# Hybrid HGRN2 and pooling block: the w_out combinations move to GpSimd's DMA queue, the staged rows load in two groups, the last two output pairs run their products in order 1 to 7

## The reference, cut to what matters

```
h = rms_norm(z)
q, fz, iv, g_hg, u, g_pool, m_hg, m_pool = split(h @ w_in + b_in)      # eight 1024-wide parts
o = hgrn2_chunkwise(q, k, iv, log_f)                                   # gated linear recurrence
y_hg   = (rms_norm(o) * silu(g_hg)) @ w_down_hg
y_pool = (pool_mix(u) * pool_scale * silu(g_pool)) @ w_down_pool
merged = sigmoid(m_hg) * y_hg + sigmoid(m_pool) * y_pool
out    = rms_norm(z + merged @ w_out)[16:]
```

## Time and profile before

| | before |
|---|---|
| median of 3 runs | 1046.86 us (1046.70, 1046.86, 1048.11) |
| time of the profiled execution | 1046.04 us |
| its span, first to last instruction | 1044.3 us |
| TensorE, matmul | 1016.9 us busy, 97% of the span |
| VectorE | 812.2 us, 78% |
| ScalarE | 510.8 us, 49% |
| GpSimd | 100.3 us, 10% |
| mean granted clock of TensorE | 0.998 |

### The profile page before, as it was taken

One profiled execution on the slowest core, in us unless ns is written; L12 is line 12 of the kernel. 1 busy time (PEld: TensorE's weight loads), 2 busy tenths in 40 slices (PEclk: granted clock), 3 DMA queues, 4 the chain that ended last, 5 costly groups with the idle time before them and its releaser, 6 DMA issues.

```text
span 1044.3 us, 18526 instructions
## 1 busy us (share of the span) xinstructions
PE 1016.9 (97%) x7204; PEld 829.0 (79%) x7204; DVE 812.2 (78%) x1319; ACT 510.8 (49%) x860; POOL 100.3 (10%) x162
## 2 busy tenths in 40 slices
PE   7999999999999999999999999999998999999996
PEld 7767888888888888878888887788776888788875
DVE  7989787868696968787666877875659879988975
ACT  7764636363636353544353433444337436435664
POOL 6200000001010101010101010011101010000130
PEclk9999999999999999999999999999999999999999
DMA  7221111111020202121312222229662384658373
GB/s 276 51 81 63 42 62 42 62 35 68 24 81 21 82 21 83 41 82 52 101 41 91 61 91 81 71 83 341 241 229 100 119 339 145 217 183 333 70 176 106
DMA packets 42630, 117.17 MB, mean 112 GB/s; under 512 B 4752, under 2 KB 4752, under 8 KB 42544
## 3 DMA queue, kind: packets, MB, share of 16 engines
q1 hardware_dynamic: 27904, 78.72, 22.8%
q0 software_dynamic: 8976, 26.26, 7.9%
q10 hardware_dynamic: 5664, 11.02, 3.0%
HBM read 86.62 MB, written 29.36 MB: 111 GB/s over the span
## 4 chain that ended last, share of the span: by engine, by line
PE 77%; DVE 14%; issue 4%; DMA 2%; ACT 2%; POOL 0%; SPq 0%; DVEq 0%; ACTq 0%
PE acc L1596 63%; PE levels L1649 2%; DVE w_lo L1872 2%; PE miscs L1671 1%; PE miscs L1683 1%; PE miscs L1682 1%; DVE r_lo L2428 1%; PE acc L1538 1%; PE levels L1596 1%; PE miscs L1478 1%; PE levels L1478 1%; DVE att L2029 1%; DMA comb_spill<-comb 1%; DVE qx L2048 1%; PE miscs L1689 1%
## 5 line engine op out<-in xcount | busy, mean ns | idle before, releaser
L1596 PE MATMUL acc<-r_hi,w_hi 128*128 128x512 f32 x1200 | 333.1, 400 | 11.8 <-ACT first L1001 4.5
L1596 PE MATMUL acc<-r_lo,w_hi 128*128 128x512 f32 x1200 | 329.5, 394 | 0.5 <-DVE r_lo L2428 0.4
L1596 PE MATMUL acc<-r_hi,w_lo 128*128 128x512 f32 x1200 | 322.2, 390 | 0.5 <-DVE w_lo L1872 0.5
L1596 PEld LDWEIGHTS acc<-r_hi,w_hi 128*128 128x128 f32 x1200 | 218.2, 188 | 61.8 <-ACT first L1001 5.4
L1596 PEld LDWEIGHTS acc<-r_lo,w_hi 128*128 128x128 f32 x1200 | 223.8, 188 | 53.8 <-issue 4.9
L1596 PEld LDWEIGHTS acc<-r_hi,w_lo 128*128 128x128 f32 x1200 | 225.5, 188 | 48.9 <-DVE w_lo L1872 1.0
L911 ACT ACTIVATE w_hi<-sum 128x512 fp32r<-128x512 f32 x164 | 102.9, 628 | 170.6 <-DVE sum L1905 91.5
L1872 DVE TENSOR_TENSOR w_lo<-sum,w_hi 128x512 fp32r<-128x512 f32 x164 | 111.9, 687 | 51.9 <-ACT w_hi L911 51.5
L1872 DVE TENSOR_TENSOR w_lo<-raws,w_hi 128x512 fp32r<-128x512 f32 x120 | 82.0, 686 | 50.0 <-ACT w_hi L911 49.9
L911 ACT ACTIVATE w_hi<-raws 128x512 fp32r<-128x512 f32 x120 | 74.6, 624 | 26.0 <-PE acc L1596 23.2
L1001 ACT ACTIVATE second<-acc,bias 128x512 f32<-128x512 f32 x31 | 21.2, 683 | 57.6 <-PE acc L1596 57.6
(11 more groups left out here) (312 smaller groups left out, 1305.2 us busy)
## 6 DMA issues: line engine op xcount, KB each, us to landing
raws<-in_wstream SPq DMA_DIRECT2D x80, 512.0 KB, 3.6
xin<-in_x SPq DMA_DIRECT2D x8, 512.0 KB, 6.3
a_spill<-gt POOLq DMA_DIRECT2D x16, 256.0 KB, 3.5
c_spill<-pg POOLq DMA_DIRECT2D x16, 256.0 KB, 2.7
stage<-a_spill ACTq DMA_DIRECT2D x4, 1024.0 KB, 15.4
comb<-in_wstream SPq DMA_DIRECT2D x4, 1024.0 KB, 5.6
smh_spill<-zq POOLq DMA_DIRECT2D x16, 256.0 KB, 3.2
comb_spill<-comb SPq DMA_DIRECT2D x4, 1024.0 KB, 4.0
```

The source lines that it names most:

```text
L1596: ins = pe.matmul(bank[:, :], weights, moving, start=n == 0 and i in (0, 1, y_first), stop=n == 3 * KH - 1, skip_group_check=True)
```

## The change

Five edits. (1) `load_comb` and `store_comb` move, unchanged but for the engine, from SyncE's queue to GpSimd's, between the gate stores of pairs 26 to 29, and the sums of the pieces move to pairs 27 to 30. (2) `load_stage(0, ...)` goes out in two groups of two, after product 3 of pairs 28 and 29, instead of four after product 3 of pair 27. (3) V5's sum moves one or two products forward (pair 30: after product 3 instead of 5; pair 34: after product 3 instead of 4). (4) In `change`, `add_22(p)` stands ahead of `operand_low(R_B21)`. (5) Pairs `OUT+2` and `FINAL` run in order 0 to 6, with the orders of the copies, additions, sums and squares on the engines to match.

```
-OUT_SUMS += [(p, s) for p in (OUT + 2, FINAL) for s in (S1, S2, S4, S3)]
+OUT_SUMS += [(p, s) for p in (OUT + 2, FINAL) for s in (S1, S2, S3, S4)]
-ORDER += [(p, i) for p in (OUT + 2, FINAL) for i in OUT_ORDER]
+ORDER += [(p, i) for p in (OUT + 2, FINAL) for i in range(PRODUCTS)]
-ADD_ORDER += [(p, c) for p in (OUT + 2, FINAL) for c in (11, 12, 22)]
+ADD_ORDER += [(p, c) for p in (OUT + 2, FINAL) for c in (11, 22, 12)]
-COPY_ORDER += [(p, c) for p in (OUT + 2, FINAL) for c in (1, 5, 2)]
+COPY_ORDER += [(p, c) for p in (OUT + 2, FINAL) for c in (1, 2, 5)]
-SQUARES += [(p, n, t) for p in (OUT + 2, FINAL) for n, t in ((0, 0), (0, 1), (1, 1), (1, 0))]
+SQUARES += [(p, n, t) for p in (OUT + 2, FINAL) for n, t in QUARTERS]
...
-COMB_AT = {(P_MH, 1): (0, 0), (P_MH, 2): (0, 1), (P_MH + 1, 0): (1, 0), (P_MH + 1, 1): (1, 1),
-           (P_MH + 1, 4): (2, 0), (P_MH + 1, 5): (2, 1), (P_MH + 2, 2): (3, 0), (P_MH + 2, 3): (3, 1)}
+COMB_AT = {(P_MM + 1, 3): (0, 0), (P_MM + 1, 4): (0, 1), (P_MH, 1): (1, 0), (P_MH, 2): (1, 1),
+           (P_MH + 1, 0): (2, 0), (P_MH + 1, 1): (2, 1), (P_MH + 1, 6): (3, 0), (P_MH + 2, 0): (3, 1)}
+COMB_DMA = {(P_MM, 3): -1, (P_MM + 1, 0): 0, (P_MH, 0): 1, (P_MH, 3): 2, (P_MH + 1, 3): 3}

 SyncE
-                if (p, n) == (P_MH, 0):
-                    load_comb(0)
-                elif (p, n) in ((P_MH, 1), (P_MH + 1, 0), (P_MH + 1, 1)):
-                    k = 2 * (p - P_MH) + n - 1
-                    store_comb(k)
-                    load_comb(k + 1)
-                elif (p, n) == (P_MH + 2, 0):
-                    store_comb(3)
 GpSimd
             for p in range(P_MM, P_DH):
                 for x in range(4):
                     store_spill(p, x)
+                    if (p, x) in COMB_DMA:
+                        k = COMB_DMA[p, x]
+                        if k >= 0:
+                            store_comb(k)
+                        if k < 3:
+                            load_comb(k + 1)
...
-            residual(OUT + 2, 0, 1)
             residual(OUT + 2, 1, 1)
+            residual(OUT + 2, 0, 1)
 ScalarE
-                    elif i == 3 and p == P_MM + 1:
-                        side_area_free(act)
-                        for x in range(4):
-                            act.wait_ge(spill_stored[x], 16 * STORES_OF[P_MM, x])
-                        for n in range(4):
-                            load_stage(0, n)
...
             for p in range(P_MH, LAST):
                 for i in range(PRODUCTS):
                     during(p, i)
+                    if p in (P_MH, P_MH + 1) and i == 3:
+                        if p == P_MH:
+                            side_area_free(act)
+                            for x in range(4):
+                                act.wait_ge(spill_stored[x], 16 * STORES_OF[P_MM, x])
+                        load_stage(0, 2 * (p - P_MH))
+                        load_stage(0, 2 * (p - P_MH) + 1)
...
             copy_first(FINAL)
+            high(POS[FINAL, 4])
+            square_z(p, 1, 1)
+            square_z(p, 0, 1)
             high(POS[FINAL, 5])
             square_z(p, 1, 0)
+            copy_second(FINAL)
+            high(POS[FINAL, 6])
+            row_left(4)
+            square_z(FINAL, 0, 0)
             copy_fifth(FINAL)
             row_left(5)
+            square_z(FINAL, 1, 1)
             square_z(FINAL, 0, 1)
             root_z(6)
             row_left(6)
 VectorE
                 use(p, 0)
+                add_22(p)
                 operand_low(f, R_B21)
                 ahead(p, 4)
-                add_22(p)
                 ahead(p, 5)
...
-                    if p == P_DH - 2 and i in (5, 6):
-                        stage_sum(0, R_V5 if i == 5 else R_V7)
+                    if p == P_DH - 2 and i in (3, 6):
+                        stage_sum(0, R_V5 if i == 3 else R_V7)
...
             low(POS[FINAL, 0])
+            add_22(OUT + 2)
+            low(POS[FINAL, 1])
             add_12(OUT + 2)
...
             write_right(5)
+            add_22(FINAL)
+            add_residual(1, 1)
+            weigh_left(7)
             add_12(FINAL)
             add_residual(0, 1)
             scale_from_root(6)
-            add_22(FINAL)
             write_right(6)
-            add_residual(1, 1)
-            weigh_left(7)
             final_quarter()
```

More of the change, by code:

```diff
@@ L842, in _, with load_comb, store_comb @@
                                    pg[:, k // 2, (k % 2) * HALF:(k % 2 + 1) * HALF]).then_inc(c_stored[k], 16)
+            out_blocks = wstream[2 * N_PAIRS:2 * N_PAIRS + 8].rearrange("(b s) p c -> s p b c", s=2)
+            def load_comb(k):
+                if k == 0:
+                    side_area_free(pool)
+                else:
+                    pool.wait_ge(S["comb_stored"], 16 * k)
+                pool.dma_start(comb[:, :, :], out_blocks[k // 2][:, :, k % 2 * HALF:(k % 2 + 1) * HALF]) \
+                    .then_inc(S["comb_loaded"], 16)
+            def store_comb(k):
+                pool.wait_ge(S["comb_made"], k + 1)
+                pool.dma_start(comb_dram[:, k // 2].rearrange("b p c -> p b c")[:, :, k % 2 * HALF:(k % 2 + 1) * HALF],
+                             comb[:, :, :]).then_inc(S["comb_stored"], 16)
             for p in range(P_MM, P_DH):
@@ L1466, in _ @@
             row_left(6)
-            square_z(FINAL, 1, 1)
             square_z(FINAL, 1, 0)
@@ L2375, in mixed, with comb_sums @@
                 dve.tensor_tensor(v, mix_banks[k], v, ALU.mult).then_inc(S["c_made"], 1)
+            def comb_sums(k, part):
+                v5_, v4_, v7_, v6_ = (comb[:, n, :] for n in range(4))
+                dve.wait_ge(S["comb_loaded"], 16 * k + 16)
+                if part == 0:
+                    steps.mark(dve.tensor_tensor(v5_, v5_, v7_, ALU.subtract))
+                    steps.mark(dve.tensor_tensor(v7_, v6_, v7_, ALU.subtract))
+                    return
+                steps.settle()
+                steps.mark(dve.scalar_tensor_tensor(v6_, v5_, -1.0, v6_, ALU.mult, ALU.subtract))
+                steps.settle()
+                dve.scalar_tensor_tensor(v4_, v6_, -1.0, v4_, ALU.mult, ALU.subtract).then_inc(S["comb_made"], 1)
             for g in range(5):
@@ L2515, in change @@
                 use(q, 0)
-            def comb_sums(k, part):
-                v5_, v4_, v7_, v6_ = (comb[:, n, :] for n in range(4))
-                dve.wait_ge(S["comb_loaded"], 16 * k + 16)
-                if part == 0:
-                    steps.mark(dve.tensor_tensor(v5_, v5_, v7_, ALU.subtract))
-                    steps.mark(dve.tensor_tensor(v7_, v6_, v7_, ALU.subtract))
-                    return
-                steps.settle()
-                steps.mark(dve.scalar_tensor_tensor(v6_, v5_, -1.0, v6_, ALU.mult, ALU.subtract))
-                steps.settle()
-                dve.scalar_tensor_tensor(v4_, v6_, -1.0, v4_, ALU.mult, ALU.subtract).then_inc(S["comb_made"], 1)
             for p in range(P_MH, P_DH - 1):
@@ L2732, in _ @@
             write_right(3)
+            token_sum(FINAL, S3)
             token_sum(FINAL, S4)
-            token_sum(FINAL, S3)
             low(POS[FINAL, 0])
+            add_22(OUT + 2)
+            low(POS[FINAL, 1])
             add_12(OUT + 2)
-            low(POS[FINAL, 1])
-            add_22(OUT + 2)
             weigh_left(4)
+            low(POS[FINAL, 2])
             low(POS[FINAL, 3])
-            low(POS[FINAL, 2])
-            low(POS[FINAL, 5])
+            low(POS[FINAL, 4])
             add_11(FINAL)
             add_residual(0, 0)
-            low(POS[FINAL, 4])
+            low(POS[FINAL, 5])
             mean_z(4)
```

55 lines of the change are left out of this document (19 added, 36 removed).

## The result

The changed kernel takes **1051.10 us** (median; 1050.07 to 1051.95), the kernel before, in the same comparison, 1046.70: ratio 1.0041 [1.0029, 1.0053]. The prediction was 1039.9, with 1037.4 to 1044.0 as its range: wrong in size and in sign. What came is close to its rival *Slower* (1049 to 1051), which had a chance of 0.07.

A forecast was written before the change was run, and what follows sets the result against it. TensorE computes 1016.9 of 1044.3 us, so only its idle time can be gained. Terms -8.28 + 0.6 + 0.5 + 1.25 + 0.4 - 1.45 = -7.0 gave median 1039.9 us, range 1037.4 to 1044.0.

The forecast's parts named there:

- Slower: Rival: GpSimd transfers over 2 us longer than SyncE's, V5's sum late, gaps in pairs 27, 29, 30; 1049 to 1051, chance 0.07.
- Comb's DMAs leave SyncE's queue: Pairs 28 to 31: raw block lands some 10 us ahead of need, TensorE's gaps go; up to -8.28 us.
- The price on GpSimd's queue: Each 512-row comb transfer takes d longer on GpSimd's queue than SyncE's; d between 0.2 and 1.8, taken as 0.8 us.
- The chain of pieces: Pairs 27 to 30: eight comb transfers in series, last store lands at 770.0, V5's sum 0.3 late; +0.5 us.
- the split `load_stage` costs nothing: Staged loads in two groups cost nothing: V5 needs the first half 35 us after its issue; four loads took 15.4.
- The gate stores at no cost: Pairs 27 to 29: gate stores wait up to 8 us behind comb DMAs, but are needed one pair (19 us) later.
- The first piece: Pair 27: load lands at 712.0, `add_22(27)` ends at 715.95, product 6 wants it at 715.44; +0.6 us.
- The operand changes: First change bound by VectorE's low parts, +1.25 us; second, VectorE idles with `add_22` first, +0.4 us.
- The end: Last two pairs in order 0 to 6 hide `add_22`; `final_quarter` starts at 1036.25, not 1037.70: -1.45 us.
- V5's sum after 771 behind comb_spill: Sign in the later profile that the forecast is wrong: V5's sum (L2437) comes after 771, waiting behind comb_spill.
- issues of comb of over 2 us: Sign in the later profile that the forecast is wrong: comb issues on GpSimd's queue take over 2 us.
- Later pieces: Rival: transfers 1.2 us or more longer on GpSimd, or staged loads hold them; TensorE stopped; 1041.8 to 1046, chance 0.18.

The follow-up runs named there:

- queue_only: Kernel before with only the comb DMAs moved to GpSimd's queue, sums and staged loads where they were: 1050.15 us, ratio 1.0041.
- three_buffers: Changed kernel with three comb buffers instead of one, the second group of staged loads waiting for stores 1 and 2: 1039.43 us, ratio 0.9931.
- after_on_sync: Changed kernel with the eight comb DMAs back on SyncE's queue at the times GpSimd issues them, still one buffer: 1060.88 us, ratio 1.0143.
- spills_first: Changed kernel with each next piece's load behind the pair's four gate stores instead of ahead of three of them: 1054.32 us, ratio 1.0075.
- stage_together: Changed kernel with all four staged loads back after product 3 of pair 27: 1049.00 us, ratio 1.0025.
- three_later_stage_later: Changed kernel with three comb buffers, first piece's sums two products later, second group of staged loads after product 6 of pair 29: 1038.17 us, ratio 0.9919.
- stage_later: Changed kernel with the two groups of staged loads later, after product 3 of pair 29 and product 0 of pair 30: 1052.53 us, ratio 1.0059.

## Why the prediction was wrong, by its steps

**Comb's DMAs leave SyncE's queue (-8.28): right as a mechanism.** The wait ahead of pair 31's weights is gone in the changed kernel and in queue_only. But taking the comb DMAs off the queue gained nothing by itself, since VectorE's waits for comb took its place; the gain came with the second buffer, and then on either queue. With three buffers pair 32 starts at 795.43, and the prediction's -8.28 + 0.6 + 0.5 on 802.61 gives 795.43 too. That agreement is partly luck: the 0.5 for V5 isn't lost there, and the timeline of three_buffers is 0.26 us late at 705 already.

**The price on GpSimd's queue (d = 0.8): too high.** It is 0.2 to 0.4; the row of 128-row issues times four was no guide, an issue of 512 rows takes 0.76 us. The Trainium skill (DMA: Bandwidth & Descriptors, Latency and other measured facts) would have given 0.4, and the traces agree with it (4.4 and 4.5 against 4.0 and 4.3 us). d wasn't the cause: without it, in after_on_sync, the eight transfers took 62.2 us.

**The chain of pieces (+0.5): this step failed.** It said that eight transfers take 38.4 us, the staged loads add about 6, d adds 6.4: 50.8. They took 61.0. With d at 0.4 this is 22.6 - 8 x 0.4 = 19.4 us more than the medians, where 6 was allowed. The last store landed at 781.8 instead of 770.0.

The neighbours of each transfer say roughly where the 19.4 went (an estimate, against 6.0 us for a load and 4.4 for a store). Store 1, store 2 and load 3 ran beside the staged loads and took 12.4, 7.0 and 8.7: 13.3 us of it. This is the term that was mis-sized, and the sentence that the split `load_stage` costs nothing looked only at V5's need of it. The other 6.1 us had no term at all. 3.9 of it is load 1, with three gate stores right behind it and a raw block just ahead (720.03). queue_only shows this part without any staged load: seven transfers 9.7 us longer than in the kernel before, of which seven times 0.4 is d.

The mistake was to take the medians of the earlier trace rows as the price of a transfer. The trace of the kernel before has another price, in its one comb load that ran beside staged loads; the view of that line shows it, and the median hides it:

```profile
L655 SPq DMA_DIRECT2D comb<-in_wstream x4: 368/373/568, 710.5 to 762.9; - x4
...
DMA to landing us min/median/max: 5.1/5.6/15.0
```

Load 0, issued at 710.5 right behind the four staged loads of 708 to 710, took 15.0 us; the other three, from 733 on, took 5.1 to 5.7. In the kernel before nobody was stopped by load 0 but VectorE for 2.5 us (its sums come at 725.5). The change puts the staged loads beside the middle of the chain, and VectorE behind each link of it. The loss then didn't fall on V5 alone (1.63 us at 785.33), where the prediction looked for it, but on every pair with a comb sum: VectorE waited 28.0 us in four places, TensorE 1.04, 1.71, 2.78, 1.70 and 1.63, and part of pair 29 ran at the lower clock.

What stays open is how a transfer's time follows from its neighbours: the runs show that it does, and no run takes the gate stores or the raw blocks away alone.

**The gate stores at no cost: held for whoever needs them, not for the chain.** From 700 to 800 us of the changed kernel no instruction waits for a gate store. But by spills_first the burst behind a load costs that load about 1 us.

**The first piece (+0.6): 1.04 in the changed kernel**, 0.55 to 1.44 in the versions with its place and with the staged loads behind it. In stage_together, where they are back in pair 27, the gaps there are 2.50 and 0.15. Load 0 took 6.9 where 6.4 was counted.

**The operand changes (+1.25, +0.4).** From pair 32's first row to the last gap of the second change the changed kernel takes 904.15 - 807.22 = 96.93 us, the kernel before 897.86 - 802.61 = 95.25: 1.7 more, where 1.65 was forecast. The size is partly luck, for the places were others: 0.73 ahead of ScalarE's copy at 813.55, then 0.40 and 0.38 at r_lo. Another 0.9 us came behind it, with a gap of 0.58 at 924.49 that no step had.

**The end (-1.45): right.** The shift against before is 998.10 - 990.89 = 7.21 us at TensorE's row that stands ahead of the last products, and 1043.56 - 1037.70 = 5.86 at `final_quarter`: -1.35. The timeline of VectorE, which answers to the earlier trace rows:

```profile
1042.90 0.75 DVE L2643 SCALAR_TENSOR_TENSOR z<-z,z_rs,fnw 128x512 f32<-128x512 f32 x1
1043.56 0.68 DVE L2659 SCALAR_TENSOR_TENSOR z<-acc,xr 128x512 f32<-128x512 f32 x1
```

**The rivals.** *Slower* had nearly the right place (the last store at 782 against its 785, losses in pairs 27, 29 and 30, besides one in 28) and the wrong reason: it decided "from d = 2", and got its small chance by d. Of the signs that the prediction named for being wrong, V5's sum after 771 behind comb_spill (781.78) and the gaps in pairs 29 and 30 came; issues of comb of over 2 us did not (0.76). The sum of *Slower* doesn't reach its place either: at d = 2 it gives 705.6 + 58.05 + 16 = 779.7, and 785 needs d = 2.7. The total of the chain decided, and d was only one of three things in it. *Later pieces* had named the other one, staged loads that hold the transfers longer, but priced it by d as well.

## What to carry to other kernels

A chain through one buffer (load, work, store, load) is priced by the sum of its transfers at the traffic of its new place, not by their medians from the old one. If the sum leaves no slack, a second buffer is worth more than a better queue: here 11 us (1051.10 to 1039.84, with the staged loads moved behind the copies) against none. Where a stretch moves, list what else moves bytes there. And a wait is paid by everything behind it on its queue: VectorE's wait for comb by a quarter, a copy and a product, ScalarE's wait ahead of a staged load by `copy_fifth`.

## What the runs showed of the hardware

On GpSimd's queue the same 1 MB store took from 4.4 us to 16.1. The long ones ran beside staged loads (store 1: 16.1 in three_later_stage_later, 12.1 from issue to landing in the changed kernel), and it fell to 7.3 in stage_later, where they had moved away. The Trainium skill (Trainium Kernel Development and Optimization, Key Constraints) says that DMAs from the three queues share the same 16 DMA engines and that several issuers only save issue time. The sums of the transfers agree (61.0 and 62.2 us for eight in series), and so do the times with three buffers (1039.43 and 1039.71 us). With one buffer the times don't (1051.10 and 1060.88), by what waits for what in SyncE's queue. Long transfers also occurred where the engines were far from full: load 1 took 9.9 us at 0.73 busy and 227 GB/s (the stretch from 721.30 above), while the stretch from 765.0 moved 415 GB/s. Why that one is so slow was not settled.
